# One half of an expert weight unit in two requests of 120 and 8 partitions, once early and once in the last group

## What is computed

```python
def expert_block(args):
    xc, gc = args
    hh = jnp.einsum("td,edf->tef", xc, w_e1) + b_e1
    glu = jnp.minimum(hh[..., 0::2], SWIGLU_LIMIT)
    lin = jnp.clip(hh[..., 1::2], -SWIGLU_LIMIT, SWIGLU_LIMIT)
    act = glu * jax.nn.sigmoid(SWIGLU_ALPHA * glu) * (lin + 1.0)
    act = act * gc[..., None].astype(act.dtype)
    return jnp.einsum("tef,efd->td", act, w_e2) + gc.astype(b_e2.dtype) @ b_e2
```

## Time and profile before

| | us |
|---|---|
| median of 3 runs | 1121.18 |
| lowest and highest of them | 1120.05, 1122.26 |
| the profiled execution, its own time | 1122.04 |
| its span in the profile | 1120.2 |
| PE busy | 1082.4 (97% of the span) |
| DVE, ACT, POOL busy | 314.7, 191.0, 141.6 |
| moved by the DMA engines | 429.13 MB, mean 383 GB/s |

### The profile page before, as it was taken

How to read it: one execution, slowest core, us unless ns; L and a number is a source line. 1 busy time by engine, 2 the same in 40 slices (tenths; PEclk the granted TensorE clock), 3 DMA queues, 4 the chain that set the end, 5 groups by cost and what they waited for, 6 DMA issues and landing times.

```text
span 1120.2 us, 13308 instructions
## 1 busy us (share of the span) xinstructions
PE 1082.4 (97%) x5048; PEld 436.8 (39%) x5048; DVE 314.7 (28%) x664; ACT 191.0 (17%) x387; POOL 141.6 (13%) x295
## 2 busy tenths in 40 slices
PE   8999999999999999999999999999999999999997
PEld 6566757533333333333333333333333233333332
DVE  4577745222222222222222222212111222222222
ACT  1154425111111111111111111110111111011111
POOL 1042300201111111111111001111111111111000
PEclk9999999999999999999999999999999999999999
DMA  8814475799999999999999999999999999999994
GB/s 264 331 38 168 153 313 231 303 428 406 430 431 430 431 431 432 431 432 432 431 432 432 435 433 432 432 432 431 432 432 431 432 432 432 430 431 430 428 428 184
DMA packets 32332, 429.13 MB, mean 383 GB/s; under 512 B 5040, under 2 KB 12496, under 8 KB 18064
## 3 DMA queue, kind: packets, MB, share of 16 engines
q1 hardware_dynamic: 29952, 427.03, 90.3%
q10 hardware_dynamic: 2352, 1.71, 0.5%
HBM read 427.67 MB, written 1.05 MB: 383 GB/s over the span
## 4 chain that ended last, share of the span: by engine, by line
PE 67%; DMA 28%; DVE 2%; ACT 1%; issue 1%; DVEq 0%; SPq 0%
DMA ring<-in_w_e_dram 28%; PE banks L725 26%; PE banks L747 15%; PE banks L315 9%; PE banks L693 4%; PE banks L666 4%; PE banks L760 2%; PE banks L297 2%; PE banks L674 1%; PE banks L386 1%; PE banks L332 1%; PE banks L538 1%; PE banks L682 1%; PE banks L348 1%; PE banks L594 0%
## 5 line engine op out<-in xcount | busy, mean ns | idle before, releaser
L725 PE MATMUL banks<-ring,xg_T 128*64 128x512 f32 x2048 | 478.0, 599 | 25.5 <-DMA ring<-in_w_e_dram 24.4
L725 PEld LDWEIGHTS banks<-ring,xg_T 128*64 128x64 f32 x2048 | 135.7, 136 | 307.6 <-issue 255.7
L747 PE MATMUL banks<-ring,act_T 128*64 128x512 f32 x1024 | 233.0, 596 | 0.9 <-DVE act_T L1946 0.9
L1918 DVE TENSOR_TENSOR x_sb<-x_sb,banks 128x1024 f32<-128x1024 f32 x64 | 78.1, 1221 | 412.7 <-PE banks L693 381.8
L747 PEld LDWEIGHTS banks<-ring,act_T 128*64 128x64 f32 x1024 | 70.3, 137 | 133.2 <-issue 127.7
L1928 DVE TENSOR_TENSOR glu<-banks,b_T 128x512 f32<-128x512 f32 x32 | 22.1, 692 | 239.1 <-PE banks L760 239.1
L1101 POOL COPY picked<-slot_table 128x2 f32 (+1 forms) x32 | 5.9, 186 | 565.5 <-PE banks L682 565.5
L693 PE MATMUL banks<-y_sb,hot_gate_T 64*128 64x512 f32 x256 | 72.0, 640 | 0.8 <-ACT y_sb L1389 0.8
L1376 ACT COPY hidden<-banks 128x1024 f32<-128x1024 f32 x32 | 32.4, 1012 | 212.7 <-PE banks L725 212.7
L1362 ACT COPY xg_rows<-banks 128x512 f32<-128x512 f32 x32 | 18.7, 585 | 264.4 <-PE banks L666 264.4
L666 PE MATMUL banks<-h_sb,hot_slot 128*64 128x512 f32 x256 | 60.4, 592 | 0.0
(11 more groups left out here) (324 smaller groups left out, 772.6 us busy)
## 6 DMA issues: line engine op xcount, KB each, us to landing
ring<-in_w_e_dram SPq DMA_DIRECT2D x82, 4096.0 KB, 37.4
ring<-in_w_e_dram SPq DMA_DIRECT2D x26, 2048.0 KB, 10.6
w_out_sb<-in_w_out_dram SPq DMA_DIRECT2D x1, 4096.0 KB, 13.2
ring<-in_w_e_dram SPq DMA_DIRECT2D x3, 1024.0 KB, 34.2
w_in_qk<-in_w_in_dram SPq DMA_DIRECT2D x1, 2048.0 KB, 24.2
w_mkv_sb<-in_w_mkv_dram SPq DMA_DIRECT2D x1, 2048.0 KB, 10.7
w_in_cq<-in_w_in_dram SPq DMA_DIRECT2D x2, 768.0 KB, 6.8
w_in_qc<-in_w_in_dram SPq DMA_DIRECT2D x1, 1536.0 KB, 23.9
```

The source lines that it names most:

```text
L725: ins = TE.matmul(PS[SLOTS * h:SLOTS * h + SLOTS, B_W1 + b, :], left, ring[slot][:, 2 * F * j:2 * F * j + 2 * F] .rearrange("p (m r) -> p ...
L747: ins = TE.matmul(PS[SLOTS * h:SLOTS * h + SLOTS, B_W2, :], actT[:, c % 4, c // 4, :], ring[slot][:, D * c + 512 * h:D * c + 512 * h + 512 ...
L1918: V.tensor_tensor(X[:, t, :], X[:, t, :], PS[:, first:first + 2, :].rearrange("p b n -> p (b n)"), ALU.add).then_inc(S("added"), 1)
```

## The change

In two places the first half of a `w_e1` unit, 128 partitions x 16 KB, is loaded by two requests in place of one: partitions 0 to 119, counted on `landed` of the buffer as before, and right behind it partitions 120 to 127, counted on a new semaphore `last_rows_landed`. The places are unit 4 of the first group and unit 12 of the last. PE waits for the new semaphore too where it begins to read these units. Since the loop body of PE is the same for each group, that wait stands in the second step of every group, for a count that is reached in the first and stays reached.

```diff
+APART = 120
...
-        def multiply_w1(i, units, c):
+        def multiply_w1(i, units, c, last_rows=lambda u: 0):
...
+            if j == 0 and last_rows(u):
+                pe.wait_ge(S("last_rows_landed"), 16 * last_rows(u))
...
+            apart = {(1, 1): 1, (GROUP - 1, 0): 2 if end else 0}
             for c in range(KC):
-                multiply_w1(i, w1, c)
+                multiply_w1(i, w1, c, lambda u: apart.get((q, u), 0))
...
+        def load_w1_half_apart(e, u, slot):
+            for rows, name in ((slice(0, APART), f"landed{slot}"), (slice(APART, P), "last_rows_landed")):
+                sp.dma_start(ring[slot][rows, 0:HALF], w1_v[e, u, rows, 0:HALF]).then_inc(S(name), 16)
...
-                        if r < W1_UNITS:
+                        if n == 4 and half == 0:
+                            load_w1_half_apart(i, r, slot)
+                        elif r < W1_UNITS:
                             load_w1_half(i, r, half, slot)
...
                 if end and n // PER_STEP == GROUP - 1:
                     for half in range(2):
-                        if r < W1_UNITS:
+                        if r == 0 and half == 0:
+                            load_w1_half_apart(w1_e, r, slot)
+                        elif r < W1_UNITS:
                             load_w1_half(w1_e, r, half, slot)
```

## The result

| | before | with the change |
|---|---|---|
| median, us | 1121.44 (4 runs) | 1136.07 (4 runs) |
| lowest and highest | 1120.05, 1122.26 | 1135.64, 1136.48 |
| span of the profiled execution | 1120.2 | 1134.9 |
| PE busy | 1082.4 | 1087.2 |

A forecast was written before the change was run, and what follows sets the result against it. DMA landings were taken to set PE's pace from roughly 600 us to its last landing wait, 1056.6 us. The early pair's -1.9 us and 0 for all else, from the median 1121.18, gave 1119.3 us; range 1118.0 to 1123.5.

The forecast's parts named there:

- The anchor: End of PE's last wait for a unit's landing, 1056.64 us; claimed that what moves it moves the program's end.
- Step 1: Early pair, first group: the engine left out loses its lag, worth -1.9 us at the anchor; bounds 0 and -3.4.
- the dry stretch: 272.7 to 274.2 us, stream nearly dry as SP's request waits for PE; claimed early engines lose their lead there.
- Step 2: The row more that eight engines carry: 0.6 us each, hidden the first time by the dry stretch, so 0.
- Step 3: Last group's pair, behind the anchor: up to 0.6 us for eight engines, under PE's slack, so 0.
- Steps 4 and 5: SP's two more issues of 0.33 us, and PE's wait for `last_rows_landed`: both hidden by queue or cover, 0 each.
- Rival B: Both pairs: a request over fewer than 128 partitions moves at half rate, +4.3 us; chance 0.15.
- Rival A: Early pair: the slow engine is not the one left out and keeps its lag, 1121.2 to 1121.8 us; chance 0.22.
- the 1.5 us that I gave a fetch: A 16 KB instruction fetch, one in 1085 to 1092 us, claimed to delay one engine by about 1.5 us, lastingly.

## Why the prediction was wrong

**The anchor was right, and with it the frame.** The end followed it, 63.5 to 63.7 us later, in the three profiles of the kernel before, with the split of columns and with the early pair alone. The sign of the change hung on how the stream moved up to it, and on what the last pair did behind it.

**Step 1, the early pair, failed twice.** It priced the pair by the share of one engine, -1.9 us, and took for granted that the other fifteen go on at 27 GB/s each. Together the engines fell to half. The pair measured +8.4 us alone. The mean rate accounts for 13.5 us at 211 GB/s in that run,

```profile
254.50:268.00 13.50, 13.50 (x64) 4.29 (x62) 1.91 (x2) 2.07 (x4) 2.45 (x6) 1.00 1.02 211
```

which is 6.9 us, less the 1.5 of the dry stretch 5.4. The mean over 240 to 340 us says the same: 400 GB/s in that run and 423 in the kernel before, 5.3 us of stream. Its profile also starts 1.0 us late (SP's request at 241.51 us, not 240.49). Of the 6.8 us between the two profiled anchors this leaves 0.5; of the 8.4 us between the medians some 3 beside the stream's loss were not separated. And the gain itself, 1.9 us, was read from one execution: in two more the slowest engine was alone for 0.6 and 1.6 us.

**Steps 2 and 3, the eight rows and the last pair.** Step 2 had 0.6 us for the eight rows, hidden; the runs put it at about 2.6 on top of the 120, with intervals too wide to say so. Step 3 put the last pair at nothing, from a slack of 2.7 us and more against 0.6. The pair alone cost 7.7 us. With it alone PE waits 1.10 us for the unit ahead and 3.33 us for the pair itself. With both pairs the unit ahead is the late one, and PE's wait of 4.8 us is for it: the rate falls to 287 GB/s at 1068 to 1070 us, while this unit lands only at 1078.9, so the pair is served and runs slowly while part of the unit ahead is still to come. I left that unit out, and there PE came only 0.9 us after the landing before (1067.32 us, against an issue at 1025.6 and 40.8 us to landing), less than at any of the places I looked at. Nor had I a term for the clock, 2.9 us. Why the unit ahead is later with both pairs than with the last alone was not separated.

**Steps 4 and 5, issues and waits, at nothing:** confirmed by the split of columns, to within its interval of 1.8 us less to 0.3 more.

**Rival B had the half rate, at a chance of 0.15, and its size was too small.** That a request of 120 rows moves at a lower rate is shown, with 224 GB/s and 204 alone. Why it does, no run shows; 112 and 16 rows, which go evenly into sixteen engines, moved at 222. I had B at +4.3 us: twice the time for the request, and nothing for its neighbours or the clock. No run shows that term, on whose weaker half the upper end of the range, 1123.5, rested; the runs showed +8.4 us for the early pair, +7.7 for the last and +14.6 for both. The rows that I held against it misled me: a load of 256 KB over 32 partitions landed in 3.0 us. Half rate adds 0.6 us to so small a load, and I judged that from a difference of two landing times, 3.0 and 5.0 us, of which at 431 GB/s only 0.6 and 2.4 us are the moving of bytes. Four times 32 partitions at full size settle it: 201 GB/s.

**Rival A, that the slow engine is not the one left out,** was not decided. In the kernel before, and again in its third profile, the halves around the last fetch landed 6.4 and 6.5 us apart: so the fetch may have hit the slowest engine. With the last pair alone, the second half into ring[3] and the two into ring[4] are:

```profile
L875 SPq DMA_DIRECT2D ring<-in_w_e_dram x1: 333/333/333, 1043.7 to 1043.7; - x1
DMA to landing us min/median/max: 47.4/47.4/47.4
```
```profile
L886 SPq DMA_DIRECT2D ring<-in_w_e_dram x2: 333/333/333, 1051.2 to 1051.7; - x2
DMA to landing us min/median/max: 45.3/47.5/49.7
```

They landed at 1091.1, 1096.5 and 1101.4 us: 5.4, then 4.9 apart. This tells nothing of the engine left out, since the kernel before does the same in its second profile: there the halves landed at 1084.2 and 1089.5 us, 5.3 apart, with the fetch in the same 7 us. So the 1.5 us that I gave a fetch is not the same in each execution either. No view shows on which engine a fetch falls, nor over how many engines the fetches are spread. Which engine is left out, and how rows are dealt to fifteen, stays open.

## What to carry to other kernels

In a stream that fills the DMA engines, as this one does, load SBUF with requests over all 128 partitions (431 GB/s here); if a transfer has to be cut, cut its columns (437) and not its partitions (135 to 224). When the DMA share is 1 and GB/s is half of its usual value (1.02 and 224 here, in place of 431), the engines are held up and do not lack work, and the shapes of the requests of that stretch are to be looked at, with those queued ahead of them. And before a gain is priced from a lag of 2 us, profile the unchanged kernel a second time, and count from a request late in the stages before, so that their variation drops out.

## What the runs showed of the hardware

- Neighbouring partitions in one request, 2 MB in all, other requests of 128 rows around: 128 rows in two requests by columns, 437 GB/s; 112 and 16, 222; 120 and 8, 211 to 224; 64, 210; 32, 201; 16, 135.
- A load of 120 rows gives 15 of the small packets that count its end, one of 8 rows gives 8, one of 128, 112, 64, 32 or 16 rows gives 16 (5040 under 512 B in the kernel before; 5054 with the change, 5039 with 120 rows alone, 5072 with 112 and 16, and 5056, 5088 and 5152 with 64, 32 and 16).
- Around a slow request the unit queued ahead of it lands late too: 47.6 us after its issue with both pairs and 43.0 with the last alone, where the last whole units of the kernel before took 39 to 41.
- After 4.8 us without a matmul the granted clock of TensorE was 0.50 from 1078 to 1084 us, and half a product took 6.46 us, not 3.60; after 3.3 us without one, in the run with the last pair alone, it was 0.50 from 1078 to 1080 us and half a product took 5.35.
- Around the last 16 KB instruction fetch the landings of two halves stood 6.4, 5.3 and 6.5 us apart in three executions of the unchanged kernel, where 4.9 is the spacing without one. In the same three the slowest engine was alone at the end for about 3, 0.6 and 1.6 us, and the spans were 1120.2, 1118.4 and 1119.2 us.
